# Half-width first units and x in single chunks, f at another offset, the order inside mean_squares, and two copies moved in mixer 1

## What is computed

```python
# first block
x = x + 0.5 * swiglu_ffn(x, ffn1)            # feed-forward 0
h = rms_norm(x, mix_norm)
ya = dsa_attention(...)                       # keys picked by an index score
yb = mlstm_branch(...)                        # conv, chunked recurrence, gates
x = x + (sigmoid(ga) * (ya @ w_proj_a) + sigmoid(gb) * (yb @ w_proj_b)) @ w_out
x = x + 0.5 * swiglu_ffn(x, ffn2)            # feed-forward 1
# second block
x = x + 0.5 * rmsnorm(swiglu(rmsnorm(x), ffn1_2), ffn1_post_g_2)   # feed-forward 2
x = x + rmsnorm(concat(moba_attention, multiscale_pool) @ w_out_2)
x = x + rmsnorm(memory_cross_attention(rmsnorm(x), rmsnorm(mem)))
x = x + 0.5 * rmsnorm(swiglu(rmsnorm(x), ffn2_2), ffn2_post_g_2)   # feed-forward 3

def swiglu_ffn(x, g, w_gate, w_up, w_down):
    h = rms_norm(x, g)
    return (jax.nn.silu(h @ w_gate) * (h @ w_up)) @ w_down
```

## Time and profile before

| | |
|---|---|
| median of 3 runs | 1130.25 us (1129.99 to 1130.55) |
| profiled execution | 1132.61 us, its span 1130.6 us |
| mean granted TensorE clock | 0.999 |
| TensorE busy | 1116.8 us, 99% of the span |
| VectorE, ScalarE, GpSimd busy | 756.0, 564.4, 45.2 us |
| DMA | 207.73 MB, mean 184 GB/s |

### The profile page before, as it was taken

How to read it: one execution, slowest core, us unless ns; L and a number is a source line. 1 busy time by engine, 2 the same in 40 slices (tenths; PEclk the granted TensorE clock), 3 DMA queues, 4 the chain that set the end, 5 groups by cost and what they waited for, 6 DMA issues and landing times.

```text
span 1130.6 us, 19589 instructions
## 1 busy us (share of the span) xinstructions
PE 1116.8 (99%) x8418; PEld 1056.3 (93%) x8418; DVE 756.0 (67%) x864; ACT 564.4 (50%) x738; POOL 45.2 (4%) x52
## 2 busy tenths in 40 slices
PE   8999999999999999999999999999999999999998
PEld 7999999988999999999999999889988987999986
DVE  6876654898977776664487666556867657655652
ACT  6544443667464554443355454445746446444441
POOL 0000000300000000000010000001201001000000
PEclk9999999999999999999999999999999999999999
DMA  8666555654455565656556575548455535765640
GB/s 303 212 205 216 189 170 161 195 165 130 130 188 175 179 220 172 203 178 198 169 198 228 157 243 181 176 140 315 143 168 175 198 112 186 224 190 184 187 148 37
DMA packets 112037, 207.73 MB, mean 184 GB/s; under 512 B 8784, under 2 KB 18256, under 8 KB 111824
## 3 DMA queue, kind: packets, MB, share of 16 engines
q1 hardware_dynamic: 109584, 198.53, 54.5%
q0 software_dynamic: 2080, 7.87, 2.1%
q10 hardware_dynamic: 288, 0.10, 0.0%
HBM read 205.42 MB, written 1.05 MB: 183 GB/s over the span
## 4 chain that ended last, share of the span: by engine, by line
PE 93%; DVE 4%; issue 1%; ACT 1%; DMA 0%; POOL 0%; SPq 0%; DVEq 0%; POOLq 0%; ACTq 0%
PE pair L455 91%; PE pair L459 2%; DVE w_lo L1465 1%; DMA x<-in_xT 0%; DVE work L1809 0%; DVE x L1657 0%; DVE xr L1491 0%; DVE top L1807 0%; DVE work L1792 0%; ACT w_hi L1056 0%; DVE dm L1838 0%; DVE dm L1778 0%; DVE den L1843 0%; DVE r_low L1519 0%; ACT xr L1071 0%
## 5 line engine op out<-in xcount | busy, mean ns | idle before, releaser
L1465 DVE TENSOR_TENSOR w_lo<-stage,w_hi 128x1024 fp32r<-128x1024 f32 (+2 forms) x376 | 452.1, 1226 | 221.0 <-ACT w_hi L1056 219.9
L1056 ACT CAST w_hi<-stage 128x1024 fp32r<-128x1024 f32 (+2 forms) x376 | 381.9, 1043 | 242.4 <-PE pair L455 230.3
L455 PE MATMUL pair<-h_hi,w_hi 128*128 128x256 f32 x1760 | 493.9, 281 | 4.1 <-DVE act_buf L1583 1.7
L455 PE MATMUL pair<-h_lo,w_hi 128*128 128x256 f32 x1760 | 490.9, 279 | 0.0
L455 PE MATMUL pair<-h_hi,w_lo 128*128 128x256 f32 x1760 | 490.9, 279 | 0.0
L455 PEld LDWEIGHTS pair<-h_hi,w_hi 128*128 128x128 f32 x1760 | 333.6, 190 | 9.6 <-issue 4.9
L455 PEld LDWEIGHTS pair<-h_hi,w_lo 128*128 128x128 f32 x1760 | 332.0, 189 | 0.0
L455 PEld LDWEIGHTS pair<-h_lo,w_hi 128*128 128x128 f32 x1760 | 330.7, 188 | 0.1
L455 PE MATMUL pair<-f_hi,w_hi 128*128 128x256 f32 x352 | 99.6, 283 | 0.0
L455 PE MATMUL pair<-f_hi,w_lo 128*128 128x256 f32 x352 | 99.6, 283 | 0.0
L455 PE MATMUL pair<-f_lo,w_hi 128*128 128x256 f32 x352 | 99.6, 283 | 0.0
(11 more groups left out here) (314 smaller groups left out, 1134.0 us busy)
## 6 DMA issues: line engine op xcount, KB each, us to landing
stage<-in_ffn_w_up SPq DMA_DIRECT2D x88, 512.0 KB, 4.6
stage<-in_ffn_w_down SPq DMA_DIRECT2D x88, 512.0 KB, 3.9
stage<-in_ffn_w_gate SPq DMA_DIRECT2D x87, 512.0 KB, 4.6
stage<-in_w_in SPq DMA_DIRECT2D x52, 512.0 KB, 4.1
stage<-in_w_out SPq DMA_DIRECT2D x16, 512.0 KB, 4.4
stage<-in_xa_wkv SPq DMA_DIRECT2D x16, 512.0 KB, 5.0
stage<-in_xa_wq SPq DMA_DIRECT2D x8, 512.0 KB, 3.8
stage<-in_xa_wo SPq DMA_DIRECT2D x8, 512.0 KB, 5.0
```

Source lines behind the costliest of these rows:

```text
L455: return e.matmul(o, l, r, start=start, stop=stop, skip_group_check=True)
L1056: e.copy(m.w_hi[u % PLACES][:, 0:w], m.stage[u % STAGES][:, 0:w]).then_inc(s.hi, 1)
L1465: e.tensor_tensor(m.w_lo[slot][:, 0:w], m.stage[u % STAGES][:, 0:w], m.w_hi[slot][:, 0:w].bitcast(F32), ALU.subtract).then_inc(s.lo, 1)
```

## The change

- The first column block of feed-forward 0 becomes twelve units: gate chunks 0 to 3 singly, up chunks 0 to 3 singly (eight units of 128 x 512), then gate 4-5 and 6-7, up 4-5 and 6-7. x comes as four single chunks, each ahead of its gate unit; chunks 4 to 7 come behind the sixth unit. ScalarE and VectorE alternate a chunk of x and a unit. mean_squares runs behind the first full unit of gate.
- f_hi and f_lo of feed-forwards 0 and 1 move from 448 to 128 within 512 bytes.
- In mean_squares the two products with one column come first, that with 256 columns last.
- Two more idle matmuls, 256 and 128 columns.
- Mixer 1, ScalarE: the copy of qT goes ahead of the four taps. VectorE: by_rank(2) goes behind the first copy of wt and the split behind it.

```diff
--- before.py
+++ after.py
@@ -88,7 +88,7 @@
 
 
 SEMS = """
-    xin0 xin1 xin2 ident par causal gain c_mix alibi poolc mem gpost out load0 load1 load2 load3 load4 load5
+    xin0 xin1 xin2 xin3 xin_rest ident par causal gain c_mix alibi poolc mem gpost out load0 load1 load2 load3 load4 load5
     hi lo used half pow zero pow2 one
     uhi ulo xT sqT fold ssum stp var std rB gr dev xbk xrow
     sq ms rt xr tr nhi nlo xup
@@ -150,8 +150,8 @@
         self.f_hi, self.f_lo, self.act_buf, self.act_rows = [], [], [], []
 
         def ffn_tiles(n, sb, buf=None):
-            self.f_hi.append(sb(f"f_hi{n}", [P, FC, S], F32R, F_REST))
-            self.f_lo.append(sb(f"f_lo{n}", [P, FC, S], F32R, F_REST))
+            self.f_hi.append(sb(f"f_hi{n}", [P, FC, S], F32R, H_REST if n < 2 else F_REST))
+            self.f_lo.append(sb(f"f_lo{n}", [P, FC, S], F32R, H_REST if n < 2 else F_REST))
             self.act_buf.append([sb(f"act_buf{n}_{i}", [P, 1024]) for i in range(2)] if buf is None else buf[0:2])
             self.act_rows.append(sb(f"act_rows{n}", [P, 1024])[:] if buf is None else buf[2])
 
@@ -271,12 +271,13 @@
                 if n == 0 and n0 == 0:
                     blocks = [Block(form, nw, 0, DC, m.h_hi, m.h_lo, p) for p in pairs[0:2]]
 
-                    self.F[0] += 1
-                    add(blocks[0], gate, 0, 0, 1)
-                    for h in range(2):
-                        for b, w in zip(blocks, (gate, up)):
-                            for k in (4 * h, 4 * h + 2):
-                                add(b, w, 0, max(k, 1) if b is blocks[0] else k, k + 2)
+                    self.F[0] += 4
+                    for b, w in zip(blocks, (gate, up)):
+                        for k in range(4):
+                            add(b, w, 0, k, k + 1)
+                    for b, w in zip(blocks, (gate, up)):
+                        for k in (4, 6):
+                            add(b, w, 0, k, k + 2)
                     continue
                 whole(gate, DC, n0, nw, form, m.h_hi, m.h_lo, pairs[0])
                 whole(up, DC, n0, nw, form, m.h_hi, m.h_lo, pairs[1])
@@ -424,13 +425,13 @@
         for parts, cols, src in srcs:
             e.dma_start(dst[parts, :, cols], src).then_inc(loads[u % STAGES], 16)
 
-    e.dma_start(m.xT[:, 0:1, :], d["xT"][:, 0:1, :]).then_inc(s.xin0, 16)
-    load(0)
-    e.dma_start(m.xT[:, 1:4, :], d["xT"][:, 1:4, :]).then_inc(s.xin1, 16)
-    for u in range(1, 4):
+    for u, sem in enumerate((s.xin0, s.xin1, s.xin2, s.xin3)):
+        e.dma_start(m.xT[:, u:u + 1, :], d["xT"][:, u:u + 1, :]).then_inc(sem, 16)
         load(u)
-    e.dma_start(m.xT[:, 4:8, :], d["xT"][:, 4:8, :]).then_inc(s.xin2, 16)
-    for u in range(4, plan.n):
+    load(4)
+    load(5)
+    e.dma_start(m.xT[:, 4:8, :], d["xT"][:, 4:8, :]).then_inc(s.xin_rest, 16)
+    for u in range(6, plan.n):
         load(u)
     for t in range(T):
         for half in range(2):
@@ -527,9 +528,9 @@
         ps = take(2)
         e.wait_ge(s.one, 2)
         e.wait_ge(s.ssum, i + 1)
-        mm(ps[:, 0:S], m.all_over_d[:], m.ssum, True, False)
         for t in range(T):
-            ins = mm(ps[:, S + t:S + t + 1], m.ssum[:, t * P:(t + 1) * P], m.all_over_d[:, 0:1], False, t == 1)
+            mm(ps[:, S + t:S + t + 1], m.ssum[:, t * P:(t + 1) * P], m.all_over_d[:, 0:1], t == 0, False)
+        ins = mm(ps[:, 0:S], m.all_over_d[:], m.ssum, False, True)
         ins.then_inc(s.stp, 1)
         free[2] = (s.var, i + 1)
 
@@ -559,7 +560,9 @@
         F, DN = plan.F[n], plan.DOWN[n]
         if n == 0:
             first_unit()
-        at = 5 if n == 0 else 3
+            for u in range(1, F):
+                scaled_unit(u, 0)
+        at = 4 if n == 0 else 3
         for j in range(8):
             scaled_unit(F + j, i)
             if j == at:
@@ -1031,6 +1034,8 @@
     e.wait_ge(s.one, 1)
     idle(512)
     idle(256)
+    idle(256)
+    idle(128)
     ffn_by_columns(0, 0, 1, 0, 2, 3)
     mixer1()
     ffn_by_columns(1, 2, 1, 0, 2, 3)
@@ -1076,7 +1081,7 @@
         if i:
             e.wait_ge(s.xT, 4 * (i - 1) + k // 2 + 1)
         else:
-            e.wait_ge((s.xin0, s.xin1, s.xin1, s.xin1, s.xin2, s.xin2, s.xin2, s.xin2)[k], 16)
+            e.wait_ge((s.xin0, s.xin1, s.xin2, s.xin3, s.xin_rest, s.xin_rest, s.xin_rest, s.xin_rest)[k], 16)
         e.activation(m.h_hi[:, k, :], m.xT[:, k, :], ACT.Copy, scale=m.col(PRE_NORMS[i], k)).then_inc(s.uhi, 1)
 
     def squares(i, p):
@@ -1252,13 +1257,13 @@
                m.pair[2][:, 0:8].rearrange("p (t pair half) -> p t half pair", t=T, half=2)).then_inc(s.ft, 1)
         hi_to(U + 20)
         relu(1)
+        hi_to(U + 21)
+        e.wait_ge(s.qkt, 1)
+        e.activation(flat(m.qT[:]), m.pair[3][:, :], ACT.Copy, scale=m.col("q_norm")).then_inc(s.qkT, 1)
         e.wait_ge(s.zero, 1)
         e.wait_ge(s.dev, 2)
         for c in range(4):
             e.activation(m.xc[:, c, :], m.xpad[:, c, 0:S], ACT.Identity, scale=m.col("conv_w", c), bias=m.col("conv_b", c)).then_inc(s.tap, 1)
-        hi_to(U + 21)
-        e.wait_ge(s.qkt, 1)
-        e.activation(flat(m.qT[:]), m.pair[3][:, :], ACT.Copy, scale=m.col("q_norm")).then_inc(s.qkT, 1)
         hi_to(U + 23)
         e.wait_ge(s.qkt, 2)
         e.activation(m.kT[:], m.pair[3][:, 0:S], ACT.Copy, scale=m.col("k_norm")).then_inc(s.qkT, 1)
@@ -1410,16 +1415,16 @@
     e.wait_ge(s.pow, 1)
     e.activation(m.stat[:, 0, 0:1], m.half_pow[:, 0:1], ACT.Square)
     e.wait_ge(s.par, 16)
-    scaled_hi(0, 0)
-    hi_to(1, 0)
-    for k in range(1, 4):
+    for k in range(4):
         scaled_hi(0, k)
-    hi_to(4, 0)
+        hi_to(k + 1, 0)
+    hi_to(6, 0)
     squares(0, 0)
-    hi_to(5, 0)
+    hi_to(7, 0)
     squares(0, 1)
+    hi_to(8, 0)
     new_norm(0, 1)
-    hi_to(9, 0)
+    hi_to(10, 0)
     ffn_by_columns(0)
     by_columns_tail(0, 1)
     mixer1()
@@ -1895,7 +1900,6 @@
         link(e.tensor_tensor(m.den[:], m.den[:], m.ft[:], ALU.max))
         linked()
         e.reciprocal(m.den[:], m.den[:]).then_inc(s.rden, 1)
-        by_rank(2, U + 26, 1, m.ga[:, 0:4, :])
         for pr in range(2):
             if pr == 1:
                 e.wait_ge(s.mav, 1)
@@ -1903,6 +1907,7 @@
             e.tensor_copy(m.wt[0][:], m.pair[3][:, 0:384]).then_inc(s.mtd, 1)
             lo_to(U + 31 + pr)
             if pr == 0:
+                by_rank(2, U + 26, 1, m.ga[:, 0:4, :])
                 pick(1, 2)
         pick(1, 2)
         picked(1)
@@ -2079,19 +2084,18 @@
     e.memset(m.ones_tile, 1.0).then_inc(s.one, 1)
     e.memset(m.all_over_d[:], 1.0 / D).then_inc(s.one, 1)
     e.wait_ge(s.par, 16)
-    scaled_lo(0, 0)
-    lo_to(1, 0)
-    for k in range(1, 4):
+    for k in range(4):
         scaled_lo(0, k)
-    lo_to(4, 0)
+        lo_to(k + 1, 0)
+    lo_to(7, 0)
     fold(0, 1)
-    lo_to(5, 0)
+    lo_to(8, 0)
     for k in range(4, 8):
         scaled_lo(0, k)
-    lo_to(6, 0)
+    lo_to(9, 0)
     fold(0, 2)
     fold(0, 3)
-    lo_to(9, 0)
+    lo_to(10, 0)
     ffn_by_columns(0, 0, 1, 0)
     by_columns_tail(0, 1)
     mixer1()
```

## The result

The changed kernel takes 1123.82 us (median of 20 runs, 1118.39 to 1131.15) against 1130.59 us for the kernel before on the same chip (20 runs, 1129.41 to 1139.58). The ratio is 0.9927 with a 95% interval of 0.9906 to 0.9947: a gain of 8.2 us, 6.0 to 10.6. (The medians are only 6.8 us apart, the means, 1132.51 and 1124.21 us, 8.3.) The forecast was a gain of 17.2 us. The profiled execution took 1124.17 us.

What follows compares the result with a forecast made beforehand. TensorE, busy 99%, bounds the kernel, so gains must come mainly from matmul pace: 3.5 + 3.5 (f), 4.3 + 4.3 (mean_squares order), 0.5 (start), 0.9 + 0.2 (mixer 1) = 17.2 us, 1130.2 to 1113.0; range 1111.2 to 1125.4.

Steps and rivals of the forecast that it cites:

- The frame: Whole kernel: TensorE busy 99%, so gains come from matmul pace, which goes along with operand place and history, not clock.
- rival (a): Feed-forwards 1 and 2: the new mean_squares order leaves the slow pace in both; gain 5.9 us, 1124.3 us; chance 0.22.
- I take quick for both: Gate and up of feed-forwards 1 and 2: new mean_squares order leaves the quick pace, 4.3 us each, little over even odds.
- f at 128: Down stages of feed-forwards 0 and 1: quick pace instead of 120.1 ns, 3.5 us each; 1.2 us at the slow pace.
- rival (e): Nothing resets the slow pace once f moves, and feed-forward 0 is slow too: +2.5 us, 1132.7 us; chance 0.04.
- The start: First units of feed-forward 0: 0.5 us gained, bounds -0.8 and 1.5; the stop grows from 1.7 to about 2.4 us.
- reaches the variances at 25.6: VectorE at the start: variances reached at 25.6 in place of 26.22, where it waited 0.52 us for TensorE.
- at the earliest: VectorE at the start: next full piece, behind the scaling of x4 to x7, split at 19.1 at the earliest, against 19.3.
- the 7.45 us that were carried over: Start, from the variances to the end of the stop: roots and first scaling take 7.45 us as now.
- Mixer 1: Mixer 1: qT copy first gains 0.9 us; earlier wt copy gains 1.0, of which 0.8 returns waiting for yb_lo, leaving 0.2.

Runs made afterwards that it cites:

- again: The changed kernel once more, no edit: 1123.93 us, ratio 0.9937 to the kernel before.
- ms_only: The kernel before with the new order inside mean_squares alone: 1130.28 us, ratio 0.9995.
- f_only: The kernel before with f of feed-forwards 0 and 1 at 128 alone: 1128.68 us, ratio 0.9973.
- after_oldms: The changed kernel with the old order inside mean_squares: 1124.08 us, ratio 0.9934 to the kernel before.
- start_only: The kernel before with the new start alone (twelve units, single chunks of x, longer idle matmuls): 1128.83 us, ratio 0.9970.
- mixer_only: The kernel before with the two copies in mixer 1 moved, nothing else: 1132.09 us, ratio 0.9995.
- reset3: Changed kernel with old mean_squares order, plus three unused matmuls streaming w_hi at 448 behind mean_squares of feed-forwards 1 and 2: 1114.80 us, ratio 0.9846 to kernel before.
- reset3_new: Changed kernel, new mean_squares order kept, plus three unused matmuls streaming w_hi at 448 behind mean_squares of feed-forwards 1 and 2: 1115.75 us, ratio 0.9840 to kernel before.

## Why the prediction was wrong, and where it was right

**The frame was right.** TensorE at 99%, two paces in one kernel at the same granted clock, and history and place as what goes with them: the 14 traces fit it. The outcome is rival (a), which was given 0.22 and 1124.3 us, a gain of 5.9 us; measured was 8.2 by the ratio and 8.8 between the traces, 5.0 of which without feed-forward 3, and 6.7 with the second block's mixers left out as well.

**The step that failed is "I take quick for both"**, for the new order in mean_squares: 4.3 + 4.3 us, half of the sum, resting on one row that went quick and one that went slow, and the earlier trace rows. Behind the new order five of six starts of a gate and up stream in feed-forwards 1 and 2 are slow (changed kernel twice, again twice, ms_only once of two); behind the old order ten of ten (before, f_only, after_oldms, start_only, mixer_only). Between the mean_squares and the stop of feed-forward 0, where nothing was added in 13 of the 14 traces, three of four are slow behind the new order and seven of nine behind the old one. So neither order brings a sure quick pace, and the old one does not bring a sure slow one. The time of ms_only, 0.9995 (0.9979 to 1.0011), excludes a gain of over 2.4 us. The slip was to take the form of the last matmul for the cause, when the prediction's own text already named the thing that reset the pace: the stretch of f. With three or twelve matmuls at those offsets, six of six streams are quick.

**What hung on that step.** With feed-forward 1 slow, f of feed-forward 1 gains 1.2 and not 3.5 us, and the 96 matmuls lose 0.3: the prediction has both numbers (1.2 in the part on f, 0.4 in (a)), and f_only shows the first alone. 8.6 + 2.3 + 0.4 = 11.3 us is by how much the sum was too high there: 17.2 - 11.3 = 5.9. The traces have 6.7 without the two rows that nothing ties to the change; the 0.8 on top are mainly the start. (The upper end of the range is a small slip in the adding: 1124.3 and the 1.3 us between the start's guess and its bad bound are 1125.6, not 1125.4.)

**f at 128** was right: 120.1 to 113.2 ns in feed-forward 0, 3.5 us in the trace, and to the slow pace, 117.6 ns, in feed-forward 1. That the new place takes away a reset was seen as well, in rival (e), at 0.04. Its first half is real: f now goes on as it finds the pace, and a slow stretch from mean_squares of feed-forward 1 to that of feed-forward 2 is 1584 matmuls long. The second half, a slow feed-forward 0, happened in one trace, of a kernel in which f still stood at 448.

**The start** was sized too low: 0.5 us, against 1.2 in the two traces' difference, 1.7 between the mean ends of the stop of four traces and ten, and 1.9 to 4.9 in the time of start_only. The prediction put the end of the stop at 33.1; it was at 32.51, and the stop is 1.3 us long and not 2.4. The error is in the step that VectorE "reaches the variances at 25.6". VectorE of the changed kernel in order of time (start, length, what; in brackets the wait ahead of it):

```profile
17.51 1.23 DVE L1470 TENSOR_TENSOR w_lo<-stage,w_hi 128x1024 fp32r<-128x1024 f32 x1 [1.15 <-ACT w_hi L1061]
20.52 4.62 DVE L1470 TENSOR_TENSOR w_lo<-stage,w_hi 128x1024 fp32r<-128x1024 f32 x4
25.06 0.42 DVE L1518 TENSOR_SCALAR xr<-pair 128x258 f32<-128x258 f32 x1
```

Its splits begin 0.55 us ahead of the earlier trace rows, the variances 1.16: the 0.52 us of waiting for TensorE are gone, as forecast, and the full split that was to end at 19.1 "at the earliest" ended at 17.51 + 1.23 = 18.74. The prediction had taken over the 16.1 us at which ScalarE has scaled x4 to x7; in the changed kernel that ends at 15.51, and the 0.55 us go through to the split. The rest, 25.06 + 7.45 = 32.51, is to the digit the 7.45 us that were carried over.

The longer idle matmuls changed something that the prediction did not rest on. TensorE of the changed kernel in order of time, first unit:

```profile
6.26 0.62 PE L456 MATMUL pair<-h_lo,w_hi 128*128 128x256 f32 x4
```

Four matmuls take 0.62 us, where the earlier trace rows have 1.05: the first unit runs at full pace, its twelve matmuls in 1.6 us instead of 2.9. It does not reach the stop, as far as the traces tell: start_only has the same idle matmuls, its first unit took 2.7 us, and its stop ended earlier than the changed kernel's, at 32.16 us.

**Mixer 1** was right: forecast 1.1, and 1.3 between the traces of mixer_only and of the kernel before, in the three places that the prediction named. ScalarE in order of time:

```profile
241.64 1.12 ACT L1262 ACTIVATE qT<-pair,par 128x1024 f32<-128x1024 f32 x1 [2.57 <-PE pair L460]
242.66 2.06 ACT L1266 ACTIVATE xr<-xpad,par 128x256 f32<-128x256 f32 x4
```

The copy now waits for TensorE instead of the other way round, and the taps follow. On VectorE the wait for wt went and the one for yb_lo came, 0.7 us for a forecast of 0.8: the price that was read from a slack of 0.2 us in the earlier trace rows. The time of mixer_only can't resolve any of this; its trace does.

**The rest**, -1.7 in the second block's mixers and +3.8 in feed-forward 3, was in no step, and nothing ties either to the change. The long stream of the second block's mixers is slow in eight of the 14 traces, ms_only and mixer_only among them, and quick in six. Feed-forward 3 is quick in the traces of ms_only, f_only, start_only and mixer_only as well, in 13 of 14 in all. It was slow in the one execution of the kernel before that was read, the trace that the forecast took as its base. Between the two traces the change is therefore worth about 5 us without feed-forward 3 and 6.7 without either, and the 8.2 us of the ratio have a remainder of 1.5 that no trace explains; a part of it may be the late starts and the slow feed-forward 0 of executions with the old start, as under mixer_only.

## What to carry to other kernels

Where a stream of equal matmuls has two paces, count matmuls per microsecond for every stretch and every trace before costing anything, then look for what stands ahead of a change from slow to quick, not for what stands ahead of the slow stretch. When an edit takes away an operation for its price, ask what that operation also reset: f at 448 cost 6.9 ns a matmul and gave back the quick pace to what followed. And one profiled execution decides nothing of the size of one such stretch: ms_only was 4.1 us shorter in its trace, and its ratio was 0.9995, and the slow feed-forward 3 of the kernel before was in no other trace.

## What the runs showed of the hardware

- Two paces of the same stream (128x256 matmuls, a weight load each) at a granted clock of 1.00: 113.3 and 117.7 ns. A stream kept its pace over up to 1584 matmuls (slow, changed kernel). It changed at groups of other small matmuls, at the stop of feed-forward 0, where nine of ten slow streams were quick behind 1.5 to 2.0 us between two starts (mixer_only's stayed slow), and at f at 448. With moving operand and weights at the same offset of 448 bytes within 512 it is 120.1 ns.
- Three or twelve matmuls of that last kind leave the quick pace, in 6 of 6 streams; three with the moving operand at 128 leave the slow one, in 2 of 2; one leaves it slow in feed-forward 1 and quick in feed-forward 2, in 2 traces of 2. Only the pair 448 and 448 was tried. Why it resets the pace, and what in TensorE holds it, no run shows: in the kernel before, a weight load starts 3 to 4 ns behind the start of the matmul ahead of it at either pace.
- Some paces are drawn again in each execution: the same code behind the same mean_squares was slow in seven of nine traces in feed-forward 0. The changed kernel's 20 times reach over 12.8 us, where one stream of 960 is worth 4.2; reset3 and reset3_new reach over 3.1 and 4.0 us in five each. That the spread of the times is made of such streams was not tested, since only one execution of each set has a trace.
- In five of 14 traces the granted clock is 0.50 (1.2 GHz) for about 3.4 us from 231 to 232 us on, behind eight small products of 1.97 us, and 128x256 matmuls are 0.21 us apart instead of 0.12. It costs 1.5 to 1.7 us.
